# Attention with two key blocks merged into one block of probabilities

## The reference

```python
dist_band = t[:, :, None] - s[:, None, :]              # s runs over the previous block and the own one
band_ok = (s[:, None, :] >= N_META) & (dist_band >= 0) & (dist_band < WINDOW)   # WINDOW = BLOCK = 128
s_band = jnp.where(band_ok[...], s_band - slopes * dist_band, -jnp.inf)
s_meta = jnp.where(meta_ok[...], s_meta - slopes * jnp.minimum(dist_meta, WINDOW), -jnp.inf)
mx = jnp.maximum(jnp.maximum(s_band.max(-1), s_meta.max(-1)), sink)
p_band, p_meta = jnp.exp(s_band - mx), jnp.exp(s_meta - mx)
denom = p_band.sum(-1) + p_meta.sum(-1) + jnp.exp(sink - mx)
o = p_band / denom @ v_band + p_meta / denom @ v_meta
```

## Time and profile before

| | us |
|---|---|
| median of 3 runs | 2664.55 (2664.0 to 2667.01) |
| the profiled execution | 2662.36 |
| its span | 2660.6 |
| the attention's query products, first to end of last | 973.53 to 1082.27 |
| end of the attention, start of the out product | 1114.09 |

### The profile page before, as it was taken

The page is one execution under the profiler, slowest core; times in us unless marked ns, Lnnn a source line. Parts: engine busy times, 40 slices in busy tenths (PEclk is TensorE's granted clock), DMA queues, the critical chain, the costliest instruction groups (busy, mean ns, idle before and its releaser), DMA issues.

```text
span 2660.6 us, 36374 instructions
## 1 busy us (share of the span) xinstructions
PE 2542.9 (96%) x13773; PEld 1881.1 (71%) x13773; DVE 1311.4 (49%) x2566; ACT 689.7 (26%) x1558; POOL 746.3 (28%) x689
## 2 busy tenths in 40 slices
PE   7999899899998999999999999999999899999998
PEld 3555784333336877687888888888877687888887
DVE  5675542211116755615558831376528615558732
ACT  2222532111104655412111101232237412111100
POOL 1421410122113400220334420234436420344320
PEclk9999999999998999999999999999999899999999
DMA  7233005699934210021222132222210021222132
GB/s 280 98 152 138 26 4 245 243 422 392 370 143 176 79 69 33 19 93 48 95 80 95 64 127 95 95 80 81 94 64 2 1 95 48 95 83 92 64 127 95
DMA packets 49644, 312.83 MB, mean 118 GB/s; under 512 B 12224, under 2 KB 14528, under 8 KB 18368
## 3 DMA queue, kind: packets, MB, share of 16 engines
q1 hardware_dynamic: 39520, 290.30, 28.3%
q0 software_dynamic: 9216, 17.85, 1.8%
q10 hardware_dynamic: 736, 2.37, 0.2%
HBM read 351.10 MB, written 16.78 MB: 138 GB/s over the span
## 4 chain that ended last, share of the span: by engine, by line
PE 74%; issue 11%; DVE 5%; POOLq 3%; ACT 2%; DMA 2%; DVEq 1%; POOL 1%; ACTq 0%
PE ps L1036 35%; PE ps L961 5%; PE ps L1269 5%; PE ps L1076 5%; PE ps L985 3%; PE ps L1338 2%; PE ps L857 2%; DMA u<-rows_in,rs 2%; PE ps L1227 2%; PE ps L1073 1%; DVE work L2099 1%; DVE work L2102 1%; PE ps L1257 1%; PE ps L1197 1%; PE ps L573 1%
## 5 line engine op out<-in xcount | busy, mean ns | idle before, releaser
L1036 PE MATMUL ps<-work,ring 128*128 128x264 f32 (+2 forms) x1228 | 285.7, 385 | 3.1 <-DVE work L2102 1.5
L2099 DVE TENSOR_TENSOR work<-work 128x128 f32<-128x128 f32 (+8 forms) x461 | 242.1, 559 | 81.6 <-ACT work L1824 24.3
L2102 DVE SCALAR_TENSOR_TENSOR work<-tmp,par,work 128x528 f32<-128x528 f32 (+1 forms) x332 | 268.0, 807 | 26.1 <-issue 1.7
L1036 PE MATMUL ps<-work 128*128 128x264 f32 (+2 forms) x1124 | 265.3, 383 | 0.0
L1036 PEld LDWEIGHTS ps<-work,ring 128*128 128x128 f32 x1228 | 233.9, 191 | 42.5 <-issue 2.7
L1036 PE MATMUL ps<-u,ring 128*128 128x264 f32 (+1 forms) x1104 | 255.3, 384 | 0.0
L1036 PEld LDWEIGHTS ps<-work 128*128 128x128 f32 x1124 | 213.5, 190 | 33.4
L1036 PEld LDWEIGHTS ps<-u,ring 128*128 128x128 f32 x1104 | 209.2, 190 | 34.0 <-issue 0.4
L3086 POOL TENSOR_TENSOR work<-ring 128x512 f32<-128x512 f32 (+1 forms) x53 | 77.7, 1466 | 529.8 <-PE ps L1036 390.7
L961 PE MATMUL ps<-work,u 128*64 128x512 f32 x640 | 169.0, 592 | 3.0 <-DMA work<-in_experts,rs 1.9
L573 PE MATMUL ps<-u,ring 128*128 128x512 f32 (+2 forms) x416 | 166.7, 554 | 3.0 <-DVE u L2096 2.9
(11 more groups left out here) (481 smaller groups left out, 4410.8 us busy)
## 6 DMA issues: line engine op xcount, KB each, us to landing
ring<-in_stream SPq DMA_DIRECT2D x169, 1024.0 KB, 4.9
work<-in_experts SPq DMA_DIRECT2D x25, 2048.0 KB, 15.0
work<-in_experts SPq DMA_DIRECT2D x25, 1024.0 KB, 16.7
ring<-in_experts SPq DMA_DIRECT2D x7, 2048.0 KB, 14.4
ring<-in_experts SPq DMA_DIRECT2D x7, 1024.0 KB, 17.3
work<-rows_out SPq DMA_DIRECT2D x4, 1024.0 KB, 7.9
h<-in_x_fm SPq DMA_DIRECT2D x1, 2048.0 KB, 19.5
rows_in<-work ACTq DMA_DIRECT2D x4, 512.0 KB, 2.6
```

The lines of the kernel that those rows point to most:

```text
L1036: m = pe.matmul(ps[:, bank, 0:n], w[kk], x[kk], start=fresh and kk == 0, stop=ends and kk == len(w) - 1, skip_group_check=not fresh)
L2099: return dve.tensor_tensor(out, x, y, op)
L2102: return dve.scalar_tensor_tensor(out=out, in0=x, scalar=s, in1=y, op0=op0, op1=op1)
```

## The change

In steps with two key blocks the two blocks of negated scores are made apart, the own block in `own_part`, and their element-wise minimum takes the previous block's place in `prob`. Exponentials, normalization and transposes then run over 16 + 128 columns in place of 16 + 256. After the transposes VectorE multiplies the turned block by a triangle of ones (`upto`) into `own_t`, and the product with v is `comb_t` times the previous v block plus `own_t` times the difference of own and previous block (`v_dif`, made once). The meta columns of both heads are turned together, and `v_meta` holds the meta rows of v padded with zeros so that each head picks its own. The transposes of a step go to one bank, 4 or 5 in turn, so a turning waits for the copies of two steps before. Normalization of step n - 1 stands behind the scaling of step n and in front of its minimum search. The query products move to passes 3, 8, 13 and so on where they stood at 4, 9, 14; the last is at pass 28. A semaphore gets another name (`tokens_scaled` to `scaled`), for the masking too.

```diff
@@ -128,8 +128,10 @@
 IN0_LOADED = [U0["in0"] + u for u in [*range(8), 12, 13, *range(8, 12)]]
 ATT = [(c, hp) for hp in range(Q_TILES) for c in (1, 2, 0, 3, 4)]
 OUT1_BANK, OUT1_EARLY = (2, 3, 7, 4, 5, 0, 1, 2), 6
-Q_HALVES = dict(zip((-1, 0, 1, 4, 6, 9, 11, 14, 16, 19, 21, 24, 26, 29), [(t, s) for t in range(1, Q_TILES) for s in range(2)]))
+Q_HALVES = dict(zip((-1, 0, 1, 3, 6, 8, 11, 13, 16, 18, 21, 23, 26, 28), [(t, s) for t in range(1, Q_TILES) for s in range(2)]))
 SCORE_BANK = [(2 * n + e) % 3 if n < 36 else 2 * (n % 2) + e for n in range(len(ATT)) for e in range(2)]
+MERGED = [sum(1 for c, _ in ATT[:n + 1] if c >= 2) for n in range(len(ATT))]
+REGION = lambda c, e: (META - 1 + (1 + META + P) * e, 1 + META + P) if c else (P + META - 1 + (1 + META) * e, 1 + META)
 SCORE_FREE = [max([0] + [i + 1 for i in range(n) if SCORE_BANK[i] == SCORE_BANK[n]]) for n in range(len(SCORE_BANK))]
 
 
@@ -365,8 +367,11 @@
         g_lru, x_lru, r_lru, i_lru, a_lru, t_lru = [at(14900 + 2 * T2 * n, 2, T2) for n in range(6)]
         w_lru = at(21300, 2, LRU, P)
         lam8 = sb("lam8", 4, LRU)
-        prob = at(23360, 3, 2, 2 + META + 2 * P)
-        prob_t = at(25008, 2, 2, 3 * P)
+        prob = at(23360, 3, 2, 2 * META + P)
+        probs = at(23360, 3, 2 * (2 * META + P))
+        own_part = at(24320, 2, P)
+        comb_t, own_t, meta_t = at(25008, 2, 2, P), at(25520, 2, 2, P), at(26032, 2, P)
+        v_dif, v_meta, v_pad = at(22400, 3, P), at(22784, 2, P), at(30284, 3 * META)
         stat = at(26544, 3, 3, 2)
         m_out = at(16900, DT, T2)
 
@@ -1144,6 +1149,9 @@
                 pe.wait_ge(sem("lru_sig"), LRU)
                 for c, (lo, n) in enumerate(CH2):
                     m = pe.transpose(ps[0:n, 4 + c // 4, c % 4 * P:(c % 4 + 1) * P], v_fm[:, lo:lo + n], ident)
+                for e in range(2):
+                    m = pe.matmul(ps[0:2 * META, 5, P * (1 + e):P * (2 + e)], v_pad[:, META * (1 - e):META * (3 - e)], ident,
+                                  start=True, stop=True)
                 m.then_inc(sem("router_done"), 1)
 
             def scores(n):
@@ -1156,46 +1164,48 @@
                     if SCORE_FREE[2 * n + e]:
                         pe.wait_ge(sem("scores_read"), SCORE_FREE[2 * n + e])
                     rows = slice(64 * e, 64 * e + 64)
-                    out = ps[0:cnt, SCORE_BANK[2 * n + e], :]
+                    out = ps[0:cnt, SCORE_BANK[2 * n + e], 0:META + 2 * P]
                     kk = k_fm[rows, hp // 4, :]
                     qq = q_fm[rows, hp, lo:lo + cnt]
-                    if c <= 2:
+                    if c == 0:
+                        m = pe.matmul(out[:, 0:META], qq, kk[:, 0:META], start=True, stop=True)
+                    elif c <= 2:
                         m = pe.matmul(out[:, 0:lo + cnt], qq, kk[:, 0:lo + cnt], start=True, stop=True)
                     else:
                         pe.matmul(out[:, 0:META], qq, kk[:, 0:META], start=True, stop=True)
                         m = pe.matmul(out[:, META:META + 2 * P], qq, kk[:, lo - P:lo + P], start=True, stop=True)
                 m.then_inc(sem("scores_done"), 1)
 
-            def key_parts(c):
-
-                return [(0, META, 0)] + [(META + P * i, P, d) for i, d in enumerate(([], [1], [1, 2], [2, 3], [3, 4])[c])]
-
             def turn(n):
                 c, hp = ATT[n]
-                cnt = CH2[c][1]
+                cnt, bank = CH2[c][1], 4 + n % 2
                 pe.wait_ge(sem("prob_ready"), n + 1)
                 if n == 0:
                     pe.wait_ge(sem("psum_read"), 1)
-                if n:
-                    pe.wait_ge(sem("prob_turned_read"), n)
-                for e in range(2):
-                    for i, (k0, kn, _) in enumerate(key_parts(c)):
-                        m = pe.transpose(ps[0:kn, 4 + e, i * P:i * P + cnt], prob[0:cnt, n % 3, e, 1 + k0:1 + k0 + kn],
-                                         ident[0:cnt, 0:cnt])
-                m.then_inc(sem("prob_turned"), 1)
+                if n >= 2:
+                    pe.wait_ge(sem("prob_turned_read"), n - 1)
+                for e in range(2 if c else 0):
+                    pe.transpose(ps[:, bank, P * e:P * e + cnt], prob[0:cnt, n % 3, e, META:META + P], ident[0:cnt, 0:cnt])
+                pe.transpose(ps[0:2 * META, bank, 2 * P:2 * P + cnt], probs[0:cnt, n % 3, META + P:3 * META + P],
+                             ident[0:cnt, 0:cnt]).then_inc(sem("prob_turned"), 1)
 
             def attend(n):
                 c, hp = ATT[n]
-                cnt = CH2[c][1]
+                cnt, b, kv = CH2[c][1], n % 2, slice(64 * (hp // 4), 64 * (hp // 4) + 64)
                 pe.wait_ge(sem("prob_turned_read"), n + 1)
+                if c >= 2:
+                    pe.wait_ge(sem("scaled"), DT + MERGED[n])
                 if n >= 2:
                     pe.wait_ge(sem("attended_read"), n - 1)
-                parts = key_parts(c)
-                kv = hp // 4
-                for i, (_, kn, vc) in enumerate(parts):
+                parts = [(lambda e: v_meta[0:2 * META, e, kv], lambda e: meta_t[0:2 * META, b, 0:cnt])]
+                if c == 1:
+                    parts.append((lambda e: v_tok[:, 1, kv], lambda e: comb_t[:, b, e, :]))
+                if c >= 2:
+                    parts.append((lambda e: v_tok[:, c - 1, kv], lambda e: comb_t[:, b, e, :]))
+                    parts.append((lambda e: v_dif[:, c - 2, kv], lambda e: own_t[:, b, e, :]))
+                for i, (w, x) in enumerate(parts):
                     for e in range(2):
-                        m = pe.matmul(ps[64 * e:64 * e + 64, 6 + n % 2, 0:cnt], v_tok[0:kn, vc, 64 * kv:64 * kv + 64],
-                                      prob_t[0:kn, n % 2, e, i * P:i * P + cnt], start=(i == 0),
+                        m = pe.matmul(ps[64 * e:64 * e + 64, 6 + b, 0:cnt], w(e), x(e), start=(i == 0),
                                       stop=(i == len(parts) - 1), tile_position=(0, 64 * e))
                 m.then_inc(sem("attended"), 1)
 
@@ -1849,6 +1859,8 @@
             act.dma_start(k_fm[HEAD:P, 0, :], k_fm[0:HEAD, 0, :]).then_inc(sem("lru_loaded"), 16)
             act.dma_start(k_fm[0:HEAD, 1, :], k_fm[HEAD:P, 1, :]).then_inc(sem("lru_loaded"), 16)
             lru_functions(LRU - 1)
+            act.wait_ge(sem("tile_done"), q + 3)
+            act.activation(v_pad[:, META:2 * META], ps[:, 2 * ((q + 1) % 2), 0:META], ACT.Copy)
             tile_copy(q + 2, v_fm, bank=q + 1)
             def query_copy(t, s):
 
@@ -1861,17 +1873,18 @@
 
             tile_copy(q + 3, q_fm[:, 0, :], scale=HEAD ** -0.5, bank=q)
             act.wait_ge(sem("router_done"), 3)
-            act.activation(v_tok[0:META, 0, :], ps[0:META, 4, 0:P], ACT.Copy)
+            act.activation(v_meta[0:2 * META, :, :], ps[0:2 * META, 5, P:3 * P].rearrange("p (e n) -> p e n", e=2), ACT.Copy)
             act.activation(v_tok[:, 1:4, :], ps[:, 4, P:].rearrange("p (c n) -> p c n", c=3), ACT.Copy)
             act.activation(v_tok[:, 4, :], ps[:, 5, 0:P], ACT.Copy).then_inc(sem("psum_read"), 1)
             query_copy(*Q_HALVES[-1])
             for n in range(len(ATT) + 2):
                 if n < len(ATT):
                     c, hp = ATT[n]
-                    cnt, nk, b = CH2[c][1], (META, META + P, META + 2 * P, META + 2 * P, META + 2 * P)[c], n % 3
+                    cnt, b = CH2[c][1], n % 3
                     act.wait_ge(sem("max_ready"), n + 1)
                     for e in range(2):
-                        x = prob[0:cnt, b, e, 0:1 + nk]
+                        lo, nk = REGION(c, e)
+                        x = probs[0:cnt, b, lo:lo + nk]
                         m = act.activation(x, x, ACT.Exp, bias=stat[0:cnt, b, 0, e:e + 1], scale=-1.0,
                                            accum_out=stat[0:cnt, b, 1, e:e + 1])
                     m.then_inc(sem("exp_ready"), 1)
@@ -1883,11 +1896,10 @@
                     act.wait_ge(sem("prob_turned"), n)
                     if n >= 3:
                         act.wait_ge(sem("attended"), n - 2)
-                    m = act.activation(prob_t[0:META, b, :, 0:cnt], ps[0:META, 4:6, 0:cnt], ACT.Copy)
                     if c:
-                        w = P if c == 1 else 2 * P
-                        m = act.activation(prob_t[:, b, :, P:P + w], ps[:, 4:6, P:P + w], ACT.Copy)
-                    m.then_inc(sem("prob_turned_read"), 1)
+                        act.activation(comb_t[:, b, :, :], ps[:, 4 + b, 0:2 * P].rearrange("p (e n) -> p e n", e=2), ACT.Copy)
+                    act.activation(meta_t[0:2 * META, b, 0:cnt], ps[0:2 * META, 4 + b, 2 * P:2 * P + cnt], ACT.Copy
+                                   ).then_inc(sem("prob_turned_read"), 1)
                 if n >= 2:
                     c, hp = ATT[n - 2]
                     lo, cnt = CH2[c]
@@ -2665,6 +2677,7 @@
                 stt(u[:, k, META:T2], h[:, k, META:T2], gain_in[:, k:k + 1], rs[:, META:T2], mul, mul).then_inc(sem("normed"), 1)
```

(54 more changed lines are left out.)

4 lines of the change are left out of this document (2 added, 2 removed).

## The result

The changed kernel takes 2676.53 us (median of 7 runs, 2671.96 to 2680.22) against 2664.97 (7 runs beside it). The ratio is 1.0041, 95% interval 1.0032 to 1.0051: slower, where 2668.5 was forecast, and above the upper end of the range (2675).

What follows compares the result with a forecast made beforehand. TensorE was taken to bound the rounds with query products, a chain through several engines the close. The terms -3.9 - 0.5 + 3.0 + 1.5 + 4 gave +4.1 us, so 2668.5 us, range 2660 to 2675.

Steps and rivals of the forecast that it cites:

- front, to the first mark: Before the query rounds: -1.3 us of transposes against +0.8 for added products and v-block differences, together -0.5.
- six rounds: Rounds with query products: each falls from 17.25 to 16.6 us, 6 x -0.65 = -3.9.
- first round of the close: Behind the last query product: VectorE's chain makes a round 12.8 us against 11.31; two rounds cost +3.0.
- rest of the close, without sums: Second of the two close rounds, again 12.8 us against 11.31 through VectorE's longer chain; both cost +3.0.
- GpSimd's sums: Attention's end: four sums beside VectorE's work hold it 7.2 us in place of 5.4; +3.6 to +5.2, taken as 4.
- wait for the differences: Out product: TensorE waits 1.5 us at its third product for differences VectorE starts later than before.
- three take 0.33 to 0.38: Turnings: three transposes, scaled from six at 0.75 us and four at 0.44, take 0.35; 1.36 saved a round.
- the walk: Query round, queues followed in time: TensorE stands 0.2 and 0.5 us behind VectorE, returning 0.7 of 1.46 saved.
- 3.6 reach the end: Attention's end before the change: sums block VectorE 5.4 us, 1.8 of it in waiting time, so 3.6 delays the end.
- VectorE is not late: Faster rival: query rounds keep the whole saving (-8.8 us), the close is even; about -6, 2658.5; chance 0.12.
- nothing at the end: Rival at the attention's end: sums hold VectorE no longer than now; 2664.5 us; chance 0.15.
- The clock rival: Slower rival: TensorE's clock is low when the out product starts, +5.6 us on the forecast, 2674; chance 0.20.

Runs made afterwards that it cites:

- a_warm1: Changed kernel with one filler product ahead of each wait of turning and of product with v from step 28 on: 2675.82 us, 1.0034.
- a_all: Changed kernel with the edits of a_end, a_warm1 and a_h together: 2666.94 us, 1.0003.
- a_noown: Changed kernel without the masking product, the product with v taking the unmasked block twice, so part of the computation differs: 2668.2 us, 1.0011.
- b_sums2: Kernel before the change with three of GpSimd's four sums moved early, behind the searches of steps 17, 22 and 27: 2664.53 us, 0.9999.
- a_end: Changed kernel with three sums early, the fourth behind the last normalization, and one warm-up product in place of four before the last turning: 2672.09 us, 1.0016.
- a_sums2: Changed kernel with three of GpSimd's four sums moved early, behind the searches of steps 17, 22 and 27: 2671.93 us, 1.0019.
- a_qold: Changed kernel with the query products put back at steps 4, 9, 14 to 29: 2673.8 us, 1.0034.
- a_normlate: Changed kernel with the normalization of the step before put back behind the minimum search: 2675.44 us, 1.0036.
- a_h: Changed kernel with eight residual products of VectorE moved from steps 4 to 11 to behind the searches of steps 7 and 12: 2674.27 us, 1.0035.
- a_nodve: Changed kernel without the masking product, the own block's scaling and the element-wise minimum, so part of the computation differs: 2661.82 us, 0.9988.
- a_warm: Changed kernel with two filler products ahead of each wait of turning and of product with v from step 28 on: 2676.61 us, 1.0037.
- a_warm1_sums2: Changed kernel with the edits of a_warm1 and a_sums2 together: 2670.35 us, 1.0015.

## Why the prediction was wrong, step by step

| step | predicted | measured |
|---|---|---|
| front, to the first mark | -0.5 | +0.4 (0.3 two more products, 0.1) |
| six rounds | -3.9 | -1.8 |
| first round of the close | +1.5 | +4.9 |
| rest of the close, without sums | +1.5 | +5.6 less the sums' part |
| GpSimd's sums | +4.0 | 1.4 to 3.5 of those 5.6 |
| wait for the differences | +1.5 | +1.3 |
| sum | +4.1 | +10.4 |

**The close round is the step that failed most, +3.4.** The sum took it for granted that TensorE keeps its clock until the sums begin. The clock was a rival only at the out product, decided there by the gap before the last turning; the fall came 37 us earlier, in gaps of 0.3 to 0.9 us a step. 2.9 us of it go with the clock (16.22 to 13.36, a_warm1; 13.37, a_all). The last 0.6 are the chain at full clock with its fillers, 13.36 for 12.8 forecast. The warm-up products before the last turning, which the forecast counted on, stood in the wrong place.

**The rounds are mis-sized, by 2.1.** The mechanism is right: waits of 0.2 and 0.5 were forecast, TensorE stands 0.52 in a round of 16.83 (16.31 busy), and a_noown gives 0.45 for the masking. What failed is "three take 0.33 to 0.38". In the chain three take 0.33 only behind a query product, else 0.48 to 0.55 (0.37 + 0.11, 0.44 + 0.11), while six had taken 0.75. So in these rows part of a turning's time doesn't go with the number of its transposes. TensorE's busy time in a round fell from 17.25 - 0.15 = 17.10 to 16.31, 0.8 and not 1.36. That leaves 17.25 - 16.83 = 0.42 a round for 0.65. The first round gained nothing (16.78 and 16.77), and the residual products, which the walk had left out, took 0.5 of the first three.

**The front** gained nothing, 9.09 and 9.15, with 0.3 on top ahead of the first query product. Where the transposes saved there went I haven't traced.

**The sums were right in kind and wrong in their base.** "3.6 reach the end" before is refuted as it stands: 0.4 (b_sums2). But with the warm-up products out of the way too, sums and warm-ups together are worth 17.13 - 12.78 = 4.35 before. In the changed kernel they are worth 22.77 - 17.05 = 5.7 without fillers (to a_end), and 23.32 - 15.44 = 7.9 with them (a_warm1 to a_all), of which a part is the clock, since in a_warm1 it stood at 0.50 for 7 us of that rest. The difference is between 1.4 and 3.5, where I took 4. With the sums out of the way and the clock at 1.00 the rest is 15.44 - 12.78 = 2.7 longer than before, with the fillers' own time in it, where 1.5 was forecast. How the measured 22.77 - 17.13 = 5.6 divide between chain, clock and sums the runs don't show more closely than that; that the forecast's 1.5 + 4 comes to about the same is in part luck, since the clock, which it left out, is in the measured one.

**The differences** came out as walked: third product 1.3 late where none was the earlier trace rows. The row of the changed kernel's out product:

```profile
L1041 PE MATMUL ps<-work,ring 128*128 128x264 f32 x48 | 11.2, 390 | 1.6 <-DVE work L2111 1.3 <-ACT work L1907 0.4
```

**Of the rivals,** "VectorE is not late" and "nothing at the end" fell with the waits of the chain and with a_sums2. The clock rival had the right cause at the wrong place. Its price of 5.6 was made of other terms (a slow start of the out product, which in fact began at 1.00), so that the clock's worth is not far from it is chance: a_end to a_all, which differ by the fillers and the residual products, is 4.3, less the 0.5 of those.

**What stays open.** What exactly makes the clock fall: the runs show that it fell at about the same place in all six kernels of the changed form without fillers and with all of VectorE's work whose rounds stayed whole (after, a_qold, a_sums2, a_end, a_normlate, a_h: 2.2 to 2.9 us behind the mark), later in a_noown and a_nodve, late in a_warm, a_warm1 and a_warm1_sums2, never in a_all; not which gap is decisive. Fillers fitted to each gap weren't tried. Each kernel has one trace, and the clock differs from one execution to the next, so a term of a few tenths may be that. Of the 16.2 us between the two profiled executions 5.8 lie outside what is counted above; 3.4 of them were there at 485 us, where the experts' stage begins and which the change doesn't reach, and 1.4 around 820 to 850, where the granted clock differed.

## What to carry to other kernels

When a change takes work from the engine that is the bound and gives it to the one that follows, cost the stretches in which that bound doesn't hold by themselves, and ask what the new idle time does to TensorE's clock there, gap by gap, not only at the next big product. The price of a small group of instructions isn't the large group's divided by its number: take it from a group of the same size. And before a stall's removal is booked, look for what stands beneath it (here warm-up products). Moved work has to land under a query product, not half a step away. And marks for comparing two traces belong on the engine that sets the pace.
